# First gates from 32 rows of the array, pooling product as four square blocks into two banks

## What is computed

```python
mod = jnp.einsum('bd,df->bf', jax.nn.silu(cond), P['w_ada'][l]) + P['b_ada'][l]
sh1, sc1, g1, sh2, sc2, g2 = jnp.split(mod[:, None, :], 6, axis=-1)
h = rmsnorm(x, P['norm1_g'][l]) * (1 + sc1) + sh1
mix, ckv, krope = mixing(h, P, l, ctx)
x = x + g1 * mix
...
for g, w in enumerate(POOL_WINDOWS):          # 4 groups of 64 channels
    ...
    diff = (mean - pf[..., sl]).astype(p.dtype)
    outs.append(jnp.einsum('bnc,cd->bnd', diff, w_pool[g]))
return jnp.concatenate(outs, axis=-1) * pool_scale
...
mixed = jnp.concatenate([out_a, out_b, out_c], axis=-1)
return jnp.einsum('bnm,md->bnd', mixed, P['w_out'][l]), ckv, k_rope
```

## Time and profile before

| what | value |
|---|---|
| median of 3 runs | 1580.99 us (1580.77 to 1581.78) |
| span of the profiled execution | 1579.1 us, 26725 instructions |
| PE busy | 1550.4 us, 98% of the span |
| VectorE, ScalarE, GpSimd busy | 561.6, 422.4, 105.7 us |
| mean DMA rate | 184 GB/s |

### The profile page before, as it was taken

How to read it: one execution, slowest core, us unless ns; L and a number is a source line. 1 busy time by engine, 2 the same in 40 slices (tenths; PEclk the granted TensorE clock), 3 DMA queues, 4 the chain that set the end, 5 groups by cost and what they waited for, 6 DMA issues and landing times.

```text
span 1579.1 us, 26725 instructions
## 1 busy us (share of the span) xinstructions
PE 1550.4 (98%) x10801; PEld 1246.5 (79%) x10801; DVE 561.6 (36%) x1335; ACT 422.4 (27%) x965; POOL 105.7 (7%) x108
## 2 busy tenths in 40 slices
PE   6999999999999999999999999999999999999998
PEld 3654545766666666544699999999999999999997
DVE  2211545765657575125774111111111111111115
ACT  2400112555645454324521111111111111111114
POOL 0006300000000000111000000000000000000010
PEclk9999999999999999999999999999999999999999
DMA  9870002000010300262477878778787787877785
GB/s 370 342 262 16 30 7 59 8 16 12 0 27 0 122 6 1 93 213 81 178 289 256 308 276 287 267 269 306 255 307 265 265 304 258 311 255 266 291 277 216
DMA packets 122475, 291.06 MB, mean 184 GB/s; under 512 B 17651, under 2 KB 19226, under 8 KB 120238
## 3 DMA queue, kind: packets, MB, share of 16 engines
q1 hardware_dynamic: 117374, 271.85, 47.7%
q0 software_dynamic: 4752, 17.30, 4.1%
q10 hardware_dynamic: 288, 1.05, 0.2%
HBM read 266.18 MB, written 21.64 MB: 182 GB/s over the span
## 4 chain that ended last, share of the span: by engine, by line
PE 95%; DVE 2%; ACT 1%; DMA 1%; issue 1%; DVEq 0%; ACTq 0%; POOLq 0%
PE ps L1223 32%; PE ps L1255 16%; PE ps L855 9%; PE ps L618 8%; PE ps L956 7%; PE ps L904 5%; PE ps L889 4%; PE ps L643 2%; PE ps L809 2%; PE ps L633 1%; PE ps L821 1%; PE ps L834 1%; PE ps L1168 1%; PE ps L650 1%; PE ps L1178 1%; PE ps L710 1%
## 5 line engine op out<-in xcount | busy, mean ns | idle before, releaser
L1223 PE MATMUL ps<-mreg,wreg 128*128 128x144 f32 x4096 | 517.1, 286 | 0.0
L1223 PEld LDWEIGHTS ps<-mreg,wreg 128*128 128x128 f32 x4096 | 508.8, 190 | 0.7 <-ACT hreg L1541 0.4
L1255 PE MATMUL ps<-mreg,wreg 128*128 128x144 f32 x2048 | 266.3, 286 | 0.0
L1255 PEld LDWEIGHTS ps<-mreg,wreg 128*128 128x128 f32 x2048 | 258.1, 190 | 0.0
L2226 DVE TENSOR_TENSOR mreg<-ps,mreg 128x144 f32<-128x144 f32 x120 | 36.9, 308 | 430.1 <-PE ps L1223 430.1
L855 PE MATMUL ps<-wreg 128*128 128x512 f32 (+2 forms) x400 | 171.7, 519 | 0.2
L1578 ACT ACTIVATE mreg<-ps 128x144 f32<-128x144 f32 x128 | 37.1, 290 | 437.4 <-PE ps L1223 437.3
L956 PE MATMUL ps<-wreg,mreg 128*128 128x512 f32 x288 | 130.8, 598 | 0.0
L618 PE MATMUL ps<-hreg,wreg 128*128 128x512 f32 (+1 forms) x400 | 128.9, 480 | 0.0
L889 PEld LDWEIGHTS ps<-const,hreg 128*128 128x128 f32 x648 | 79.9, 141 | 58.8 <-issue 39.3
L1837 DVE TENSOR_REDUCE stat<-ps 128x1 f32<-128x1280 f32 (+1 forms) x72 | 97.7, 1357 | 57.4 <-PE ps L855 57.3
(11 more groups left out here) (300 smaller groups left out, 1154.0 us busy)
## 6 DMA issues: line engine op xcount, KB each, us to landing
wreg<-in_w_e_dram SPq DMA_DIRECT2D x96, 2048.0 KB, 11.8
wreg<-in_w_ada_dram SPq DMA_DIRECT2D x16, 1024.0 KB, 8.2
wreg<-in_w_ada_dram SPq DMA_DIRECT2D x16, 512.0 KB, 10.9
wreg<-in_x_sample_dram SPq DMA_DIRECT2D x8, 512.0 KB, 4.7
wreg<-in_w_out_dram SPq DMA_DIRECT2D x1, 4096.0 KB, 12.9
x_rows<-wreg SPq DMA_DIRECT2D x8, 512.0 KB, 2.8
xn_rows<-wreg SPq DMA_DIRECT2D x8, 512.0 KB, 2.8
wreg<-x_rows SPq DMA_DIRECT2D x8, 512.0 KB, 9.3
```

The lines of the kernel that those rows point to most:

```text
L1223: mm = pe.matmul(o[:, 0:CAP], w[s][:, k, (f % 4) * P:(f % 4 + 1) * P], xsT[b][:, k, :], start=(k == 0), stop=(k == KD - 1))
L1255: mm = pe.matmul(bank[4 + dm % 2][:, 0:CAP], w2[f // 4][:, f % 4, dm * P:(dm + 1) * P], hidT[:, f, :], start=(f == 0), stop=(f == 7))
```

## The change

The first gates' products read only 32 of the 128 rows: rows 32 * hf to 32 * hf + 31 of the one-hot column and of mod_rows. Two jobs that follow each other use different rows of the array and different banks.

The pooling jobs are renamed ("pool", j, g) and come group of tokens by group. For each group PE issues four products of 64 x 64 at the job j = 0, after it has waited for both banks; the job j = 1 issues nothing. Block (m, jj) reads rows 64 * jj and writes partitions 64 * m of the bank of job jj, so bank j holds channel groups j and j + 2. The semaphore steps twice, behind the third and the fourth product. Because mixT's two pooling tiles thereby hold the channels in another order, the scale vector and four blocks of rows of w_out are loaded in that order.

```diff
-    jobs += [("pool", m, g, "A") for m in range(2) for g in range(3)]
+    jobs += [("pool", j, g, "A") for g in range(3) for j in range(2)]
...
-                                (V_PS, pool_scale[0], 2), (V_QN, q_norm_g[0], 3), (V_KN, kv_norm_g[0], 2)):
+                                (V_QN, q_norm_g[0], 3), (V_KN, kv_norm_g[0], 2)):
                 sp.dma_start(vecs[row:row + n, :], src.rearrange("(n p) -> n p", p=P)).then_inc(vecs_in, 16)
+            sp.dma_start(vecs[V_PS:V_PS + 2, :].rearrange("j (m p) -> j m p", m=2),
+                         pool_scale[0].rearrange("(m j p) -> j m p", m=2, j=2)).then_inc(vecs_in, 16)
...
-            sp.dma_start(w_out_sb, w_out[0].rearrange("(k p) f -> p k f", p=P)).then_inc(w_out_in, 16)
+            for k0, k1 in ((0, 2), (4, KD)):
+                sp.dma_start(w_out_sb[:, k0:k1, :],
+                             w_out[0, k0 * P:k1 * P, :].rearrange("(k p) f -> p k f", p=P)).then_inc(w_out_in, 16)
+            for m in range(2):
+                sp.dma_start(w_out_sb[64 * m:64 * m + 64, 2:4, :],
+                             w_out[0, (2 + m) * P:(3 + m) * P, :].rearrange("(j p) f -> p j f", j=2)).then_inc(w_out_in, 16)
...
                     cnd, hf = job[1], job[2]
+                    rows = slice(32 * hf, 32 * hf + 32)
                     row = 32 * hf + cnd
-                    mm = pe.matmul(o, ident[:, row:row + 1].to_broadcast([P, P]), mod_rows,
+                    mm = pe.matmul(o, ident[rows, row:row + 1].to_broadcast([32, P]), mod_rows[rows, :],
                                    start=True, stop=True)
...
-                    m, g = job[1], job[2]
-                    if (m, g) == (0, 0):
+                    j, g = job[1], job[2]
+                    if (j, g) == (0, 0):
                         pe.wait_ge(small_in, 16 * 10)
                         pe.wait_ge(diff_ok, 2)
                     gn, at = GROUPS[g][1], FLAT_AT[g]
-                    mm = pe.matmul(o[:, 0:gn], w_pool_sb[:, m, :], win_sum[2 * m][:, at:at + gn],
-                                   start=True, stop=True)
+                    if j == 0:
+                        evicted(pe, BEFORE[n + 1])
+                        for m in range(2):
+                            for jj in range(2):
+                                rows = slice(64 * jj, 64 * jj + 64)
+                                mm = pe.matmul(bank[BANK[n + jj]][64 * m:64 * m + 64, 0:gn], w_pool_sb[rows, m, rows],
+                                               win_sum[2 * m][rows, at:at + gn], start=True, stop=True)
+                                if m == 1:
+                                    mm.then_inc(job_mm, 1)
+                    continue
...
-                        pe.wait_ge(w_out_in, 16)
+                        pe.wait_ge(w_out_in, 16 * 4)
```

## The result

The changed kernel takes 1614.89 us in the median of six runs (1608.19 to 1622.33), the kernel before 1581.11 in six runs beside them: a ratio of 1.0211, 95% interval 1.0189 to 1.0234, some 34 us slower. The forecast was 1579.6 with a range to 1582.2. It was wrong, and wrong in a place that it never looked at.

The account below looks back on a forecast made before the run. PE was taken to bound the kernel, with 95% of the chain. Gates -1.4, pool 0 and loads 0 took the span from 1579.1 to 1577.7; 1.9 carried over gave 1579.6 us, range 1578.2 to 1582.2.

Parts of the forecast that it names:

- What bounds the kernel: Whole kernel: PE holds 95% of the chain of waits, so an edit counts only where PE or what it awaits shortens.
- First gates: First gates' products: pairs on different array rows run at once, 3.44 us becoming 2.03 with switching, a gain of 1.4.
- The estimate from the Trainium skill: First gates: four row tiles listed at 3.07 times one tile, so a gain of 0.9 us in place of 1.4.
- Rival (a): Gates and pooling: row tiles don't share the array, only column tiles do; gates lose 0.3 us, total 1581.3; chance 0.12.
- Pooling product: Pooling stage before the rotary product: PE's work shrinks by nearly 2 us but becomes waiting for VectorE, so worth 0.
- (b): Pooling stage: the twelve small products run one after another; with the gates' 0.3, +2.9 us, total 1583.9; chance 0.05.
- (d): Pooling stage: its gain reaches the end too, 5.3 us shrinking to some 2.2, total 1576.5 us; chance 0.04.
- a loss is possible: Pooling stage: it could lose time only if the product outlasts its cover; no gain, since VectorE sets the rotary product's start.
- the 0.8 us of cover: Pooling stage: slack between the pooling product's end at 254.24 us and VectorE freeing the rotary product's bank at 255.07.
- Rival (c): Rotary product behind pooling: PE's idle time lowers the clock, costing 3 us if half runs at half speed; chance 0.06.
- The loads: Scale vector in four pieces, output weights in four transfers: covered by 0.8 and 68 us of slack, so cost 0.

## Why the prediction was wrong, point by point

**What bounds the kernel: right, but read too near the change.** PE holds the chain, so the two edited places were read with care. The expert loop, about half of the kernel, was left out because the diff doesn't touch it. The diff does move it: everything behind the pooling product lies 28 instructions further on.

**First gates: right.** Forecast 1.4 us, measured 1.33. Two row tiles do share the array: 1.72 + 0.13 = 1.85 us was the forecast for the eight passes, 1.91 was measured, and 0.20 more for the passes behind them, against 0.18. The estimate from the Trainium skill, "TensorE: Matmul & The Clock Gate", Part 3, a gain of 0.9, was too low here. Rival (a) is out.

**Pooling product: right as to the engine, and this is the step that failed.** The third group begins 1.20 us ahead of the rotary product, forecast 255.09 - 253.89 = 1.20; the last wait for VectorE is 0.75, forecast 0.8. The gain is 0, the blocks run side by side, rivals (b) and (d) are out. But "the pooling edit is worth 0" was reached by counting passes by their time in the array. They were never counted as code, and the claim "a loss is possible" was bounded by the 0.8 us of cover. The step has a second price, which the runs put at +35 us for the 28 instructions alone (1616.18 against 1581.1), and at 0 for the same change with its loop at another place in a piece.

**Rival (c), the clock: given too little.** It came true in the profiled run, 1.67 us where 3 was named. The argument against it took the end of the kernel, where the clock held some five microseconds of idle time. The rows of after show it at 0.57 in 253 to 257 us, behind waits of 2.16 and 0.75 us with 0.45 us of work between, so what held at one place was no bound for another. Nor is the fall certain: one profiled execution with the same waits kept 1.00. The clock at the router's end is left open: in 766 to 776 us it reads 1.00 before and 0.66 after, but 0.83 in the kernel before with 28 small products, which has no changed pooling, and 1.00 in the changed kernel with one turn written out.

**The loads: right.** The out-projection, which reads the output weights, stands still for nothing but "issue" in its weight loads, 54.0 us after and 54.1 before. PE's first product now waits for the scale vector, the last of the small loads, but until 9.52 us where it waited until 9.57. With the loop moved the whole change is at 1580.0.

**The range.** The cases that were priced lay within 4.3 us of it, since all of them were about the two edited places. None could have given 1615.

**What the fetches say of the mechanism.** A loop of 6.5 pieces turns without a single fetch where it begins at 34.20 (44 pieces in all, and no packet in 1018 to 1515 us) and misses where it begins at 34.31. The places that are good are those where the loop's pieces and one piece read ahead come to eight: from 34.20 to its end at 40.70 it touches pieces 34 to 40, with 41 eight. If the engine is fed a little ahead of what it runs, then a loop that ends at 40.81 already reaches into piece 41 and calls for 42, the ninth. The kernel before fits this: it fetches its next piece at 1515.4 to 1518 us, right behind the branch at 1515.4 that leaves the loop, where it first runs on past 40.70. At 37.34 and 40.60 the loop ends at 43.85 and 47.11 and needs nine as well. The Trainium skill, "Runtime: NRT & Kernel Launch", section "Instruction fetch mechanics", gives TensorE 128 KiB for its code, 2048 instructions, refilled first in, first out by blocks of 16 KiB, which is eight pieces. All thirteen kernels agree with that, if one piece is read ahead. The same section also speaks of two cache lines only (worked out there for 32 KiB), and of a stall at each taken branch whose target is outside a window of two pages; by that every turn of 6.5 pieces would have stalled before the change too, and the trace shows no stall (0.0 us of idle time at line 1223, branches of 0.22 us). Which piece is thrown out, and why the first branches miss in some runs and not in others near the point, no trace here shows: that the loop and what is read ahead must fit into eight pieces is argued from the counts. What the runs do show is that the loop's place alone makes and unmakes the loss.

## What to carry to other kernels

An edit that adds instructions also moves all the code behind it on that engine: before calling it free, work out in how many pieces of code a hot loop behind it lies, and compare the instruction queue's packet count before and after (44 against 80 here, in a queue that takes 0.4% of the DMA engines' time). Here a wait for "issue" at the first instruction of a loop, with the queue's packets up and the branch's record at 6.7 us, meant that the loop's code no longer stayed in. Moving the loop by instructions that cost nothing, here satisfied waits beside long products, brought it back. And work taken out of a stage that waits for another engine turns into idle time; in three of four profiled executions the next products ran at a lower clock behind it.

The best of these kernels are the gates alone (0.9987, interval 0.9978 to 0.9996) and the whole change with its loop moved and the idle time filled (0.9991, 0.9981 to 1.0000). Their intervals overlap: no gain of the pooling half shows here.

## What the runs showed of the hardware

- One missed branch back on TensorE costs 4.7 to 5.3 us of standing still in five of the six kernels that miss, 14.4 us for four in the sixth, and in those five 1.6 to 3.1 us more, since the 32 passes behind it, partly at the lower clock, take 5.7 to 7.2 us in place of 4.1. Why one place in the program is cheaper than another is open.
- Each miss fetches nine pieces of 16 KB, not one: the whole turn is fetched again (62, 80, 86 and 89 packets, all a multiple of nine above the program's own). At the first miss after the change two packets come in 1030 to 1034 us, in the stop, and seven in 1034 to 1130, in the turn behind it; the turn whose branch hit (1227 to 1337 us) brings none.
- Four instructions, from 20 to 24, are the distance between no miss and two of five, in one profiled run of each.
- Two row tiles of 32 rows and 512 columns run at 1.91 us for eight passes where one behind another took 3.44: 1.80 times.
